# The recurrence of a time-mixing layer: four turned arrays and one product on ScalarE's banks, the product at another place

## The chip, the cores and the metric

One core of a Trainium2 chip. The metric is the device time of one execution in microseconds (us). Engines: TensorE (PE in the profile; PEld its weight loads), VectorE (DVE), ScalarE (ACT), GpSimd (POOL) and SyncE (SP), which issues DMAs.

## The reference, cut to what matters

The kernel computes one inference step of a two-layer hybrid decoder for 272 prompt tokens (16 of them learned) and 8 sample tokens. The change lies in the second layer, in the RWKV-7 recurrence over the prompt's 272 tokens, with 8 heads of 64:

```python
def wkv7(r, w, k, v, a, b, S0):
    def step(S, inp):
        r_t, w_t, k_t, v_t, a_t, b_t = inp
        sa = jnp.einsum('bhij,bhj->bhi', S, a_t)
        S = S * w_t[:, :, None, :] + sa[..., None] * b_t[:, :, None, :] + v_t[..., None] * k_t[:, :, None, :]
        return S, jnp.einsum('bhij,bhj->bhi', S, r_t)
```

The kernel does not step through tokens. It works by tiles of tokens: inside a tile the coupling of the tokens through `a` and `b` is a triangular system, whose inverse is built by doubling, and the state `S` goes forward by chunks of 32 tokens.

## The kernel before

Each engine has its own program; semaphores join them. All results of TensorE land in PSUM. Four banks (`VB`) are emptied by VectorE and four (`AB`) by ScalarE. Each set is a ring: TensorE's `claim()` takes the next bank and waits until it was freed four claims ago; `close(ring, ins, name)` tells the emptying engine that a bank is full and remembers under `name` the count at which it will be free again; `until(name)` waits for that. The emptying engine calls `take()` in the same order, so the order of an engine's emptying is that of TensorE's closing in its ring. On VectorE each step waits for its own end (`s.do`). `empty` (L1765 for VectorE, L2158 for ScalarE) copies one bank to scratch. In the profile, L1769 is VectorE's copy in `empty`, L1772 `mul`, L1775 `add`, L2160 ScalarE's copy.

The recurrence (TensorE from L543, VectorE from L937, ScalarE from L1150) runs over three tiles of 128, 128 and 16 tokens. Per tile:

- L546: four arrays (`ATF`, `BLF`, `KLF`, `XV`) are transposed to token rows, one bank each, and copied to `ATK`, `BLK`, `KLK`, `VTK` by VectorE. In tile 0 only, TensorE then transposes the shift rows (`sho`, L552, four banks of ScalarE), and VectorE waits for their copies before it writes `AKT`.
- L564: five pairs of products, a pair for even and odd heads, which VectorE masks into `NTM`, `TM_`, `AKT`, `RBT`, `RKT` (ten multiplications). Six more steps form the initial `TM_` and `TTM` (`t_init`), for which TensorE waits; GpSimd starts the sample rows' recurrence (L1238 on) from tile 0's.
- L567 to L588, four levels: for each parity a product `x` (L576) that VectorE masks into `XX`, then from it an update of `TM_` (L583, not in the last level) and one of `TTM` (L587, `t0` and `t1`), which VectorE adds.
- L590 to L593: `ak`, the strictly lower triangle `AKT` times the values `VTK`, 8 products in one bank that VectorE copies to `AK`.
- L594 to L601: after `until("t1")`, `ta` = `TTM` times `ATK`, and `tv` = `TTM` times `AK` (L600).
- L606: `re`. L620: per chunk of 32 tokens the products that become `GTM` and `CCM`; VectorE forms `GTM[:, c]` by a multiplication of a constant identity with a column of `PL`, then copies and adds from the bank.
- L629, L630, L638, L642: output and state, chunk by chunk; ScalarE copies the tile's output (`yw`, L1152). Then the next tile starts.

Behind the three tiles TensorE goes on with the attention of the same layer.

## Time and profile before

| | |
|---|---|
| median of 3 runs | 1148.06 us (1147.82, 1148.06, 1151.13) |
| profiled execution | 1146.33 us, span of its records 1144.6 us |
| PE busy | 988.4 us (86%) |
| DVE busy | 484.6 us (42%) |
| ACT busy | 216.3 us (19%) |
| POOL busy | 138.0 us (12%) |
| mean granted TensorE clock | 0.879 |
| the recurrence | 583.0 to about 737 us of the span |

Times in the trace are microseconds from the start of the span. Each row of a timeline merges equal instructions of one engine that follow one another: start, duration, engine, line, operation, tiles, shape, count, and in brackets how long the engine stood idle before it and what released it. Ends of matmuls are modelled, so that two rows of PE can overlap a little. PEclk is the granted TensorE clock: 1.00 is 2.4 GHz, 0.50 is 1.2 GHz.

### The profile page before, as it was taken

To read this page: it belongs to the slowest core of one execution; us is meant where nothing else is said; L and a number is where in the kernel's file an instruction comes from. 1 tells how busy PE (TensorE), PEld (TensorE's weight loads), DVE (VectorE), ACT (ScalarE), POOL (GpSimd) and SP (SyncE) were. 2 spreads that over 40 slices of the span, in tenths; PEclk is the share of its full clock that TensorE was granted. 3 is DMA by queue.
4 is the path that set the end of the run, shared out by engine and by line. 5 is a ranking of instruction groups with operands and counts; after the bars stand their busy time and mean duration, and the time that the engine had idled before them with its cause. 6 is when DMAs were issued, how large, how long until landed. Compare 5 with 4: busy or idle time off the path is not lost.

```text
span 1144.6 us, 17771 instructions
## 1 busy us (share of the span) xinstructions
PE 988.4 (86%) x7132; PEld 742.6 (65%) x7132; DVE 484.6 (42%) x1060; ACT 216.3 (19%) x462; POOL 138.0 (12%) x177
## 2 busy tenths in 40 slices
PE   6997478779799999899969778996888988999995
PEld 4775366557666666677759777754555767666674
DVE  1697723452431110214886675438663135111114
ACT  0112011201401101125520000031454032111103
POOL 0005001000040000000029600002720002200000
PEclk9998756779699999989989688596699987999998
DMA  9403101715169998032100100003722541999501
GB/s 310 168 24 37 34 1 42 265 42 198 60 254 385 394 400 242 1 120 89 53 14 1 40 1 2 7 1 113 204 64 74 184 184 51 376 389 398 220 1 38
DMA packets 77222, 156.88 MB, mean 137 GB/s; under 512 B 19605, under 2 KB 57549, under 8 KB 68215
## 3 DMA queue, kind: packets, MB, share of 16 engines
q1 hardware_dynamic: 67668, 148.28, 35.6%
q0 software_dynamic: 3760, 4.48, 1.8%
q10 hardware_dynamic: 5710, 2.96, 0.9%
q8 instruction: 58, 0.95, 0.3%
q14 instruction: 26, 0.21, 0.1%
HBM read 149.25 MB, written 5.27 MB: 135 GB/s over the span
## 4 chain that ended last, share of the span: by engine, by line
PE 70%; DVE 21%; DMA 3%; ACT 3%; issue 2%; SPq 0%; POOL 0%; DVEq 0%; ACTq 0%
PE bank L1686 10%; PE bank L1350 7%; DVE scratch L1772 7%; PE bank L1673 6%; PE bank L1746 5%; PE bank L1718 5%; PE bank L1603 5%; DVE scratch L1775 2%; PE bank L1464 2%; PE bank L576 2%; PE bank L1634 2%; PE bank L756 2%; DMA scratch<-u_tok_dram 1%; PE bank L1552 1%; PE bank L587 1%
## 5 line engine op out<-in xcount | busy, mean ns | idle before, releaser
L1350 PE MATMUL bank<-x_fm,weight_slots 128*128 128x280 f32 x576 | 143.0, 411 | 4.2 <-ACT x_fm L2228 2.8
L1350 PEld LDWEIGHTS bank<-x_fm,weight_slots 128*128 128x128 f32 x576 | 112.5, 196 | 32.9 <-issue 4.4
L2160 ACT ACTIVATE scratch<-bank 128x280 f32<-128x280 f32 (+5 forms) x118 | 52.9, 454 | 325.1 <-PE bank L1718 92.3
L1686 PE MATMUL bank<-weight_slots,scratch 128*64 128x256 f32 x672 | 92.5, 379 | 1.2 <-DVE scratch L1769 1.2
L1686 PEld LDWEIGHTS bank<-weight_slots,scratch 128*64 128x64 f32 x672 | 58.5, 137 | 27.8 <-issue 4.6
L1769 DVE COPY scratch<-bank 128x256 f32<-128x256 f32 (+5 forms) x108 | 55.9, 517 | 43.1 <-PE bank L1673 17.2
L1772 DVE TENSOR_TENSOR scratch<-scratch 128x64 f32<-128x64 f32 (+12 forms) x95 | 57.8, 626 | 33.9 <-ACT scratch L2160 31.4
L1673 PE MATMUL bank<-scratch 128*128 128x128 f32 x512 | 68.3, 289 | 0.0
L1772 DVE TENSOR_TENSOR scratch<-bank,scratch 128x256 f32<-128x256 f32 x16 | 6.8, 424 | 143.6 <-PE bank L1686 143.6
L1603 PE MATMUL bank<-scratch,weight_slots 128*128 128x280 f32 x256 | 63.5, 411 | 4.0 <-DVE scratch L1772 4.0
L1673 PEld LDWEIGHTS bank<-scratch 128*128 128x128 f32 x512 | 62.2, 199 | 4.1 <-issue 0.4
L1746 PE MATMUL bank<-scratch 128*128 128x280 f32 x256 | 60.9, 400 | 1.4 <-ACT scratch L2160 1.4
L1603 PEld LDWEIGHTS bank<-scratch,weight_slots 128*128 128x128 f32 x256 | 50.2, 197 | 17.0 <-DVE scratch L1772 4.4
L1746 PEld LDWEIGHTS bank<-scratch 128*128 128x128 f32 x256 | 48.5, 190 | 14.7 <-ACT scratch L2160 3.2
L1686 PE MATMUL bank<-scratch 128*64 128x256 f32 x352 | 56.9, 379 | 0.0
L1263 POOL DMA_DIRECT2D scratch<-in_cache_krope x64 | 34.4, 538 | 160.9 <-DVE residual L1017 143.6
L1686 PEld LDWEIGHTS bank<-scratch 128*64 128x64 f32 x352 | 35.7, 137 | 16.4 <-issue 3.4
L1207 POOL TENSOR_TENSOR scratch<-scratch 128x256 f32<-128x256 f32 x24 | 16.1, 704 | 241.3 <-DVE scratch L1772 241.3
L1464 PE MATMUL bank<-scratch 64*42 64x128 f32 x128 | 25.9, 418 | 22.1 <-DVE scratch L1775 22.1
L1718 PE MATMUL bank<-weight_slots,scratch 128*64 128x512 f32 x192 | 43.8, 598 | 0.3
L2221 ACT ACTIVATE scratch<-residual 128x280 f32<-128x280 f32 x32 | 11.7, 437 | 156.6 <-DVE residual L2018 156.6
L1772 DVE TENSOR_TENSOR scratch<-bank,consts 128x512 f32<-128x512 f32 (+5 forms) x69 | 33.7, 488 | 15.4 <-PE bank L576 11.7
(380 smaller groups left out, 1496.3 us busy)
## 6 DMA issues: line engine op xcount, KB each, us to landing
weight_slots<-in_moe_w_down SPq DMA_DIRECT2D x24, 1024.0 KB, 9.5
weight_slots<-in_moe_w_up SPq DMA_DIRECT2D x22, 1024.0 KB, 7.9
weight_slots<-in_moe_w_gate SPq DMA_DIRECT2D x20, 1024.0 KB, 7.2
scratch<-in_moe_w_gate SPq DMA_DIRECT2D x12, 1024.0 KB, 8.2
scratch<-in_moe_w_up SPq DMA_DIRECT2D x10, 1024.0 KB, 8.8
weight_slots<-in_od_w_in SPq DMA_DIRECT2D x9, 1024.0 KB, 5.8
weight_slots<-in_ev_w_in SPq DMA_DIRECT2D x8, 1024.0 KB, 11.9
scratch<-in_moe_w_down SPq DMA_DIRECT2D x8, 1024.0 KB, 10.0
```

Of the source, the lines that this page charges most:

```text
L576: ins = pe.matmul(heads(b, r)[:r, hp, :], NTM[:r, par, hp, 0:r], TM_[:r, par, hp, 0:r], start=True, stop=True)
L1263: pool.dma_start(CK[:, sm, pg, 256:288], a["cache_krope"][bass.ds(page[i], 1), 0].rearrange("o p c -> p (o c)")).then_inc(ev(f"cache_krope ...
L1350: ins = pe.matmul(b[:, 0:NT], w[:, k, P * m2:P * m2 + P], src[:, k, :], start=(k == 0), stop=(k == kt - 1))
L1464: ins = pe.matmul(b[0:HCOL, P * i:P * i + P], HS[lo:lo + SP_N, j, g // 2, :], CP[lo:lo + SP_N, j, g // 2, 1:CL + 1, :].rearrange("p l c -> ...
L1603: ins = pe.matmul(b[:, 0:NT], w[:, k0 + k, P * m2:P * m2 + P], src[:, k, :], start=(which == 0 and k == 0), stop=(which == 1 and k == 3))
L1673: ins = pe.matmul(b[:, f], XTM[:, t, 4 * half + c, :], slots(t, slice(0, P)), start=False, stop=(t == 1))
L1686: ins = pe.matmul(b[CAP * j:CAP * j + CAP, 0:DE], XG[:, q % 2, k, CAP * j:CAP * j + CAP], w[j][:, k, :], start=(k == 0), stop=(k == KD - 1))
L1718: ins = pe.matmul(b[CAP * j:CAP * j + CAP, :], HT[:, q % 2, f, CAP * j:CAP * j + CAP], w[j][:, f, 512 * h:512 * h + 512], start=(f == 0), ...
L1746: ins = pe.matmul(b[:, 0:NT], YG[:, q, P * m:P * m + P], DSPT[:, q, :], start=(q == 0), stop=(q == NQ - 1))
L1769: s.do(dve.tensor_copy(dst, src if len(dst.shape) == 2 else src.rearrange("p (a b) -> p a b", a=dst.shape[1])), v_free)
L1772: return dve.tensor_tensor(o, x, y, ALU.mult)
L2160: return act.activation(dst, b[:rows, 0:width], f, **kw).then_inc(ring.free, 1)
```

## The change

The four transposed arrays of each tile go to ScalarE's ring: TensorE claims from `A`, and ScalarE empties them, in tile 0 between its copies of the sample rows and those of the shift rows. `ak` goes to ScalarE's ring too, and TensorE computes it in level 0 of each tile, behind the two `x` products and ahead of what uses them, after a new wait for the copies of the turned arrays (`until("wkv_tok")`). VectorE's five copies per tile fall away. The number of instructions stays the same otherwise.

```diff
--- before.py
+++ after.py
@@ -541,10 +541,10 @@
             n_st = 0
             for tt, (c0, r) in enumerate(PT):
                 for src in (ATF, BLF, KLF, XV):
-                    b = V.claim()
+                    b = A.claim()
                     for m in range(4):
                         ins = pe.transpose(b[:r, P * m:P * m + P], src[:, m, c0:c0 + r], ident)
-                    close(V, ins, "wkv_tok")
+                    close(A, ins, "wkv_tok")
                 if tt == 0:
                     for q in range(0, RT_N, 4):
                         b = A.claim()
@@ -575,6 +575,12 @@
                         for hp in range(4):
                             ins = pe.matmul(heads(b, r)[:r, hp, :], NTM[:r, par, hp, 0:r], TM_[:r, par, hp, 0:r], start=True, stop=True)
                         close(V, ins, f"x{par}")
+                    if lev == 0:
+                        until("wkv_tok")
+                        b = A.claim()
+                        for h in range(WH):
+                            ins = pe.matmul(b[:r, WD * h:WD * h + WD], AKT[:r, h % 2, h // 2, 0:r], VTK[:r, WD * h:WD * h + WD], start=True, stop=True)
+                        close(A, ins, "ak")
                     for par in range(2):
                         until(f"x{par}")
                         if lev < 3:
@@ -587,10 +593,6 @@
                             ins = pe.matmul(heads(b, r)[:r, hp, :], XX[:r, par, hp, 0:r], TTM[:r, par, hp, 0:r], start=True, stop=True)
                         close(V, ins, f"t{par}")
 
-                b = V.claim()
-                for h in range(WH):
-                    ins = pe.matmul(b[:r, WD * h:WD * h + WD], AKT[:r, h % 2, h // 2, 0:r], VTK[:r, WD * h:WD * h + WD], start=True, stop=True)
-                close(V, ins, "ak")
                 until("t1")
                 for src, name in ((ATK, "ta"), (AK, "tv")):
                     if name == "tv":
@@ -935,9 +937,6 @@
                 s.do(mul(BON[:, m, :], b[:, 0:NT], XV[:, m, :]), v_free)
             n_st = 0
             for tt, (c0, r) in enumerate(PT):
-                for dst in (ATK, BLK, KLK, VTK):
-                    empty(dst[:r, :], 512, r)
-
                 def heads(b, n):
                     return b[:n, 0:4 * n].rearrange("p (h x) -> p h x", h=4)
 
@@ -965,7 +964,6 @@
                             s.do(add(TM_[:r, par, :, 0:r], TM_[:r, par, :, 0:r], heads(b, r)), v_free)
                         b = V.take()
                         s.do(add(TTM[:r, par, :, 0:r], TTM[:r, par, :, 0:r], heads(b, r)), v_free)
-                empty(AK[:r, :], 512, r)
                 empty(TA[:r, :], 512, r)
                 empty(TV[:r, :], 512, r)
                 b = V.take()
@@ -1144,10 +1142,14 @@
 
             for q in range(6):
                 empty(SROW2[0:NB, 512 * q:512 * q + 512], 512, rows=NB)
-            for q in range(0, RT_N, 4):
-                n = P * min(4, RT_N - q)
-                empty((SHO1 if q < 8 else SHO2)[0:NB + 1, P * (q % 8):P * (q % 8) + n], n, rows=NB + 1)
             for tt, (c0, r) in enumerate(PT):
+                for dst in (ATK, BLK, KLK, VTK):
+                    empty(dst[:r, :], 512, rows=r)
+                if tt == 0:
+                    for q in range(0, RT_N, 4):
+                        n = P * min(4, RT_N - q)
+                        empty((SHO1 if q < 8 else SHO2)[0:NB + 1, P * (q % 8):P * (q % 8) + n], n, rows=NB + 1)
+                empty(AK[:r, :], 512, rows=r)
                 b = A.take()
                 act.activation(YW[:, :, c0:c0 + r], b[:, 0:4 * r].rearrange("p (h x) -> p h x", h=4), ACT.Copy).then_inc(a_free, 1)
             for h in range(MH):
```

## Rows read from the trace of the kernel before

**Rows 1.** The page's chain of work that ended last, shares of the span by engine.

```profile
PE 70%; DVE 21%; DMA 3%; ACT 3%; issue 2%; SPq 0%; POOL 0%; DVEq 0%; ACTq 0%
```

**Rows 2.** Timeline, TensorE: start us, us, engine, line, operation, count, [idle before, releaser].

```profile
583.03 1.91 PE L546 MATMUL bank<-consts,scratch 128*128 128x128 f32 x16
...
586.39 2.06 PE L564 MATMUL bank<-scratch 64*128 64x128 f32 x32
...
648.54 3.67 PE L546 MATMUL bank<-consts,scratch 128*128 128x128 f32 x16
...
712.32 0.37 PE L564 MATMUL bank<-scratch 64*16 64x16 f32 x16
...
713.75 0.86 PE L564 MATMUL bank<-scratch 64*16 64x16 f32 x32 [1.06 <-DVE scratch L1769]
```

**Rows 3.** Timeline, VectorE, the heads of the three tiles.

```profile
587.66 7.22 DVE L1772 TENSOR_TENSOR scratch<-bank,consts 128x512 f32<-128x512 f32 x10 [1.06 <-PE bank L564]
...
653.84 1.42 DVE L1772 TENSOR_TENSOR scratch<-bank,consts 128x512 f32<-128x512 f32 x2 [0.82 <-PE bank L564]
...
710.78 2.82 DVE L1769 COPY scratch<-bank 16x512 f32<-16x512 f32 x4 [1.31 <-PE bank L546]
...
713.63 2.58 DVE L1772 TENSOR_TENSOR scratch<-bank,consts 16x64 f32<-16x64 f32 x10
```

**Rows 4.** Timeline, ScalarE, ahead of tile 0.

```profile
581.04 2.98 ACT L2160 ACTIVATE weight_slots<-bank 8x512 f32<-8x512 f32 x6 [3.59 <-PE bank L537]
```

**Rows 5.** Timeline, TensorE, level 0 of tile 0 and of tile 2.

```profile
599.33 3.75 PE L576 MATMUL bank<-scratch 128*128 128x128 f32 x16 [6.05 <-DVE scratch L1775]
...
602.87 1.91 PE L583 MATMUL bank<-scratch 128*128 128x128 f32 x8
...
718.54 0.39 PE L583 MATMUL bank<-scratch 16*16 16x16 f32 x8 [0.16 <-DVE scratch L1772]
```

**Rows 6.** Timeline, TensorE, behind the last level of tiles 0 and 2.

```profile
622.79 1.90 PE L592 MATMUL bank<-scratch 128*128 128x64 f32 x16
...
624.52 3.74 PE L600 MATMUL bank<-scratch 128*128 128x64 f32 x32
...
724.57 1.86 PE L592 MATMUL bank<-scratch 16*16 16x64 f32 x16
...
726.23 3.62 PE L600 MATMUL bank<-scratch 16*16 16x64 f32 x32
```

**Rows 7.** Timeline, VectorE, last addition to TTM in tiles 0 and 2.

```profile
623.06 0.69 DVE L1775 TENSOR_TENSOR scratch<-scratch,bank 128x512 f32<-128x512 f32 x1 [0.43 <-PE bank L587]
...
724.84 0.21 DVE L1775 TENSOR_TENSOR scratch<-scratch,bank 16x64 f32<-16x64 f32 x1 [0.28 <-PE bank L587]
```

**Rows 8.** Timeline, VectorE: forming GTM in tile 0, and once in tile 1.

```profile
635.50 0.56 DVE L1772 TENSOR_TENSOR scratch<-consts,scratch 128x256 f32<-128x256 f32 x1
...
637.01 1.09 DVE L1772 TENSOR_TENSOR scratch<-consts,scratch 128x256 f32<-128x256 f32 x1
...
639.05 1.53 DVE L1772 TENSOR_TENSOR scratch<-consts,scratch 128x256 f32<-128x256 f32 x1
...
698.97 0.42 DVE L1772 TENSOR_TENSOR scratch<-consts,scratch 128x256 f32<-128x256 f32 x1
```

**Rows 9.** Timeline, GpSimd, the sample rows' recurrence beside tile 0.

```profile
635.86 1.96 POOL L1247 TENSOR_TENSOR scratch<-scratch 128x1024 f32<-128x1024 f32 x1
...
637.90 2.40 POOL L1248 TENSOR_TENSOR residual<-residual,scratch 128x1024 f32<-128x1024 f32 x1
...
640.38 2.41 POOL L1249 TENSOR_TENSOR scratch<-residual,scratch 128x1024 f32<-128x1024 f32 x1
```

**Rows 10.** Timeline, TensorE, chunk products and first state step of tile 0.

```profile
633.71 1.01 PE L620 MATMUL bank<-scratch 32*64 32x64 f32 x41 [1.63 <-issue]
...
641.55 1.12 PE L638 MATMUL bank<-scratch 64*64 64x64 f32 x16 [3.17 <-DVE scratch L1775]
```

**Rows 11.** Windows: us, then PE, PEld, DVE, ACT, POOL busy, PEclk, DMA, GB/s.

```profile
632.00:634.00 2.00, 0.37 (x27) 0.29 (x28) 0.00 (x0) 0.00 (x0) 1.92 (x2) 0.65 0.00 0
```

## The prediction

> **What bounds the kernel now.** I read the page's chain first: TensorE holds 70% of it and VectorE 21% [rows 1]. Then the timeline of each engine over the recurrence, 583 to 741 us of the profile, in which three tiles (128, 128 and 16 tokens) run one after another. Three things are to be seen there.
>
> At the head of a tile, TensorE transposes (L546), then makes the products (L564), and VectorE empties the transposes and masks the products. VectorE was idle 1.06 us before the masks of tile 0 and 0.82 us before those of tile 1, and what it waited for was L564 [rows 3]. So the four copies of the turned arrays are over by then, and VectorE waits for TensorE. Only in tile 2 is it the reverse: copies from 710.78 to 713.60, masks at 713.63 with no idle [rows 3], and TensorE's L564 stood 1.06 us for a bank that a copy held [rows 2].
>
> In the levels TensorE works without a break. In tile 0 L583 starts (602.87) while the modelled end of L576 is at 603.08, with no idle shown [rows 5]; tile 1 repeats this. Before level 0, however, it stands 6.05 us for VectorE's masks and initial arrays [rows 5], and no part of the change shortens these.
>
> Behind the levels, `ak` (L592) starts as soon as the last L587 has been issued, and `ta` (L600) follows it [rows 6], while VectorE makes the last addition to TTM, on which `ta` depends, beside `ak` [rows 7]. So `ak` is now the cover of a latency.
>
> **The change part by part.** The profiled execution took 1146.33 us (span 1144.6, 1.7 us around it), the median of the three runs is 1148.06. I add the difference found in the trace to the median.
>
> (a) *Turned arrays to ScalarE.* VectorE loses four copies a tile. In tiles 0 and 1 this is worth 0: TensorE's start of L564 isn't held by them (no idle on its rows at 586.39 [rows 2]), and the masks follow L564. What covers them is TensorE's own work between the first transpose and the first product; without that cover the four would cost 2.82 us [rows 3]. In tile 2 the first mask could start where L564's first pair ends, 712.69 [rows 2], plus about 0.24 us (the distance from one engine's end to the other's start at the head of tile 0: its first 16 of 32 rows, half of 2.06 us, end at 587.42, mask at 587.66 [rows 2, 3]): 712.93 instead of 713.63, 0.70 us. But then the products come just in time. Four VectorE banks hold two pairs; the third pair waits for two masks of 0.258 us [rows 3] and needs 0.43 us itself (0.86 for two [rows 2]), so that masks 5 and 9 each come some 0.24 us late. I take a gain of 0.22, with 0 and 0.70 as bounds.
>
> On ScalarE's side, tile 0: its six copies of the sample rows run from 581.04 to 584.02, 0.50 us each [rows 4]; the four new ones end near 586.1, and only then is a bank free for the last of the `sho` transposes, which TensorE is ready to start at about 586.2. The products come behind it in program order. I take 0.1 us, bounds 0 and 0.3. The `sho` copies end near 588.2, while VectorE asks for them only at its fifth mask, 590.5 (587.66 plus four of 0.72 [rows 3]): no cost. In tiles 1 and 2 ScalarE has nothing else; its bank of `yw` is free before the fourth transpose claims it. The SP stores behind `sho` move 1 us later and nobody waits for them. The added wait for `wkv_tok` stands long after these copies: no cost.
>
> (b) *`ak` behind x0 and x1 of level 0.* There TensorE has no gap, so all of it is inserted: 1.73 us in tile 0 (622.79 to 624.52 [rows 6]), the same in tile 1. Both level 0s start at half clock, since 16 of L576 take 3.75 us and then speed up; I take the point where the clock rises as fixed in time, so that some of `ak` runs slow, and as much of L583 and L587 runs fast in its stead. In tile 2, 1.66 us (724.57 to 726.23 [rows 6]) less the idle of 0.16 and the pipelining there: about +1.42.
>
> (c) *`ak` gone from behind the levels.* The sum would be zero if the cover weren't lost. The last addition ends at 623.75 (623.06 + 0.69 [rows 7]), and TensorE can be at `ta` 0.10 us later, 623.85. Before, TensorE was free at 622.79 [rows 6]. So 1.06 us of the 1.73 come back as a stall: tile 0 +1.06, tile 1 +1.06. Tile 2: addition ends 725.05, `ta` at 725.15 instead of 726.23, -1.08, with (b) +0.34. VectorE's copy of `ak` vanishes between two waits for TensorE: 0. What is late next is `ta`, `tv`, `re` and the chunk products, all 1.06 us later.
>
> (d) *A step in tile 0 that turns 1.06 into 2.5.* After the products of the chunks VectorE forms GTM four times by a multiplication whose two inputs both lie in scratch and constants. In tile 1 one takes 0.42 us; in tile 0, beside GpSimd, 0.56, 1.09 and 1.53 [rows 8]. Against GpSimd's rows the rule is exact: the one begun at 637.01 ends at 638.10, 0.28 us after GpSimd's end at 637.82; the one begun at 639.05 ends at 640.58, 0.28 after 640.30 [rows 8, 9]. The one at 635.50 ends at 636.06, just as GpSimd's next begins at 635.86. So each waits for the GpSimd instruction that is under way. The next multiplication begins 0.95 us after the end of one, and TensorE's state step 0.97 us after the last (640.58 to 641.55 [rows 8, 10]). Now everything 1.06 later, GpSimd where it is (it started from tile 0's initial arrays, which don't move against it): the second begins at 636.56 and ends at 638.10, the third 639.05 to 640.58, the fourth begins at 641.53 and waits for GpSimd's end at 642.79 (640.38 + 2.41 [rows 9]), ends at 643.07, state step at 644.04. That is +2.49 in place of +1.06. It holds for any shift between 0.28 and 2.3 us.
>
> The Trainium skill ("SBUF — State Buffer", section "SBUF: two separate sides") says that VectorE and GpSimd share a port pair held for a whole instruction, that a VectorE operation with two SBUF inputs takes part in it, and that the loser fully blocks. The trace agrees, with the 0.28 us above each time; a notion of shared bandwidth would stretch the multiplications by a ratio and leave tile 0 at +1.06.
>
> Sum: 0.1 + 2.49 (tile 0), 1.06 (tile 1), 0.34 - 0.22 (tile 2) = +3.8 us, so 1148.06 + 3.8 = 1151.8. With the bounds of (a) it is +3.3 to +4.1; TensorE's clock adds more than that, since its full level comes and goes in this region. It fell inside the window 632 to 634 us (mean 0.65 [rows 11]) and tile 1's transposes ran at half level (3.67 us against 1.91 [rows 2]). A rise or fall one us earlier or later costs or gives half a us, and there are some five in the region: I allow 1.2 us to either side, 1150.6 to 1153.0. By the Trainium skill ("TensorE: Matmul & The Clock Gate", "What's actually happening") the monitor runs free and does not restart with the kernel, so the same code may get its clock at another point; no run shown here tells that.
>
> **The rivals.**
>
> 1. *Tile 0's step (d) doesn't come.* TensorE stands 1.63 us with no releaser in the middle of L620 [rows 10]. If that gap shrinks by over 0.8 us, the second multiplication begins early enough to end at 636.06 as before and tile 0 costs 0.1: +1.3, 1149.4. If the multiplications don't queue as I read them, tile 0 costs 1.16: +2.3, 1150.4. For: the gap has no cause in the profile. Against: nothing ahead of it changes in number, and the multiplications' ends fit three times.
> 2. *The half clock lasts longer.* A TensorE idle of 1.06 us behind the levels and a longer one before the state steps could keep the clock low further into tile 1's levels. A full-clock level lasts 5.6 us (L576 of level 0 alone took 3.75 at the half clock), so one more us to a whole level at half speed costs 1 to 2.8 more: 1152.8 to 1154.6. Against: before L576 TensorE stands 6.05 us anyway.
> 3. *The other side, by the clock.* If the gap in L620 vanishes, TensorE may stay busy enough to keep full clock past 632. Then tile 1's transposes take 1.91 in place of 3.67 (-1.8), four state steps (L638 took 1.12 us in the first [rows 10]) perhaps 0.4 less each, the first products 0.4 less: -3.8 together. With tile 0 at +0.1 and tiles 1 and 2 at +1.2 that is -2.5: 1145.6. [...] Little speaks for it.
> 4. *The relief reaches the path.* If VectorE's copies were what holds the tiles, -2.8 three times and -0.7 for each of two `ak` copies, against what (b) and (c) show: up to -9.8, 1138.3. The idle of 1.06 and 0.82 us before the masks [rows 3] speaks against it.
>
> **How the numbers follow.** Forecast 0.50; rival 1 0.24; rival 2 0.17; rival 3 0.05; rival 4 0.04. A measurement here tells 0.3% from no change, 3.4 us: the limit 1151.5 lies inside the forecast's own range, and I put 0.19 of its 0.50 below it. Faster: rival 4 and a part of 3, 0.05. Same: 0.19 + 0.24 + 0.04 = 0.47. Slower: 0.31 + 0.17 = 0.48. The range 1148.6 to 1154.6 takes in the forecast and rivals 1 and 2, and leaves out 3 and 4.
>
> **What would show it.** Masks start as late after L564 as before in tiles 0 and 1, and VectorE's idle before them grows by the copies. L583 of level 0 starts 1.7 us later after L576. Between the last L587 and `ta` TensorE idles about 1.0 us for VectorE. GTM's last multiplication of tile 0 ends 0.28 us behind a GpSimd end, and the state step starts about 2.5 us later than before. Wrong would be: masks that start earlier, `ak` that finds a gap, or a clock that falls elsewhere.

## The result, and the profile after

The changed kernel takes 1158.16 us in the median of 13 runs, against 1148.67 us for the kernel before in 13 runs beside them. The two medians lie 9.5 us apart; the ratio estimated from all these runs is 1.0068 [1.0049, 1.0087], which is 7.8 us (5.6 to 10.0), and by it I go. I had forecast 1151.8 us, 3.7 us more than the median then known. The sign was right, the size (+3.8 us) was half of what came, and the time lies above the range.

Two things make the profiles hard to read here. Executions of the kernel before spread from 1141.51 to 1154.04 us. And its code ahead of the recurrence, which the change doesn't touch, took 583.03 us in the profile before and 586.49 us after. So I compare stretches, not absolute times, and below I use four profiles of each kind where one could mislead.

The page of the changed kernel: busy time of the engines, and the shares of the chain of work that ended last (before: [rows 1]).

```profile
PE 996.2 (87%) x7132; PEld 748.8 (65%) x7132; DVE 474.9 (41%) x1045; ACT 224.1 (19%) x477; POOL 138.1 (12%) x177
PE 71%; DVE 22%; ACT 3%; issue 2%; DMA 2%; SPq 0%; DVEq 0%
```

VectorE has lost 9.7 us of work and ScalarE has 7.8 us more, as the change says. The chain still runs through TensorE. TensorE itself is 7.8 us longer busy with the same number of matmuls, and that is already the hint: the same matmuls take longer where the granted clock is lower.

TensorE's timeline in tile 0 of the changed kernel (start us, us, line, shapes, count, idle before with its releaser):

```profile
586.49 1.91 PE L546 MATMUL bank<-consts,scratch 128*128 128x128 f32 x16
...
589.86 2.06 PE L564 MATMUL bank<-scratch 64*128 64x128 f32 x32
...
602.80 3.75 PE L576 MATMUL bank<-scratch 128*128 128x128 f32 x16 [6.05 <-DVE scratch L1777]
606.35 3.51 PE L582 MATMUL bank<-scratch 128*128 128x64 f32 x16
609.65 2.02 PE L589 MATMUL bank<-scratch 128*128 128x128 f32 x8
...
630.70 3.79 PE L602 MATMUL bank<-scratch 128*128 128x64 f32 x32 [0.85 <-DVE scratch L1777]
...
648.80 1.12 PE L640 MATMUL bank<-scratch 64*64 64x64 f32 x16 [4.95 <-DVE scratch L1777]
```

The products (L564) start 3.37 us after the transposes, before 3.36 [rows 2]. `ak` (L582) now stands in level 0, whole, and for 3.51 us: the clock is at its half level there. Then `ta` (L602) has the stall that was expected, 0.85 us. From `ta` to the first state step it is 18.10 us, before 17.03 (624.52 to 641.55 [rows 6, 10]). From the first `x` to `ta` it is 27.90 us, before 25.19 [rows 5, 6].

VectorE's masks at the heads of the three tiles, changed kernel:

```profile
591.12 7.22 DVE L1774 TENSOR_TENSOR scratch<-bank,consts 128x512 f32<-128x512 f32 x10 [4.98 <-PE bank L564]
...
660.93 7.22 DVE L1774 TENSOR_TENSOR scratch<-bank,consts 128x512 f32<-128x512 f32 x10 [5.32 <-PE bank L564]
...
720.48 2.58 DVE L1774 TENSOR_TENSOR scratch<-bank,consts 16x64 f32<-16x64 f32 x10 [2.43 <-PE bank L564]
```

The idle before the masks was 1.06 and 0.82 us [rows 3] and is 4.98 and 5.32 now: what the copies and the waits between them took has become idle time of VectorE. In tiles 0 and 1 they had not been on the path.

### The profile page after: what moved, and what is told of

It is laid out like the page before. It is cut to its first block, busy times and chain, and to the rows that moved or that the text cites. A ratio compares the mean times of both kernels' runs of the same rounds, so it can differ in the third digit from the quotient of the medians.

```text
span 1151.6 us, 17759 instructions
## 1 busy us (share of the span) xinstructions
PE 996.2 (87%) x7132; PEld 748.8 (65%) x7132; DVE 474.9 (41%) x1045; ACT 224.1 (19%) x477; POOL 138.1 (12%) x177
## 4 chain that ended last, share of the span: by engine, by line
PE 71%; DVE 22%; ACT 3%; issue 2%; DMA 2%; SPq 0%; DVEq 0%
PE bank L1688 10%; DVE scratch L1774 7%; PE bank L1352 7%; PE bank L1675 6%; PE bank L1748 5%; PE bank L1720 5%; PE bank L1605 5%; DVE scratch L1777 3%; PE bank L1466 2%; PE bank L576 2%; PE bank L1413 2%; PE bank L1636 2%; PE bank L758 2%; PE bank L1554 1%; PE bank L593 1%
## 5 line engine op out<-in xcount | busy, mean ns | idle before, releaser
L2162 ACT ACTIVATE scratch<-bank 128x280 f32<-128x280 f32 (+5 forms) x133 | 61.1, 468 | 369.8 <-PE bank L1720 92.3
L1771 DVE COPY scratch<-bank 128x256 f32<-128x256 f32 (+6 forms) x93 | 45.6, 490 | 37.8 <-PE bank L1675 16.9
```

Source lines behind the costliest of these rows:

```text
L1771: s.do(dve.tensor_copy(dst, src if len(dst.shape) == 2 else src.rearrange("p (a b) -> p a b", a=dst.shape[1])), v_free)
L2162: return act.activation(dst, b[:rows, 0:width], f, **kw).then_inc(ring.free, 1)
```

## The experiments

Columns of the table: the ratio to the kernel before with its 95% interval; the stretch of the recurrence in the profiled execution, from the first transpose (L546) to the first matmul of the next stage (`pe.matmul` on `uk`, L662 before and L664 after); and the stretch from there to the end of the span.

| kernel | edit | ratio | recurrence, us | behind it, us |
|---|---|---|---|---|
| before | | 1 | 154.8 | 406.8 |
| after | | 1.0068 [1.0049, 1.0087] | 158.7 | 406.4 |
| e1 | before again | 1.0005 [0.9982, 1.0027] | 153.3 | 406.9 |
| e2 | after again | 1.0072 [1.0046, 1.0098] | 155.9 | 410.4 |
| e3 | turned arrays alone | 0.9993 [0.9965, 1.0021] | 152.9 | 407.3 |
| e4 | `ak` alone | 1.0083 [1.0054, 1.0113] | 161.5 | 410.8 |
| e5 | after, `ak` in level 1 | 1.0054 [1.0031, 1.0078] | 160.7 | 410.5 |
| e6 | after, `ak` ahead of level 0 | 0.9960 [0.9938, 0.9982] | 149.3 | 409.0 |
| e7 | e6, `ta` even heads first | 0.9954 [0.9929, 0.9978] | 151.9 | 406.3 |
| e8 | after, `ta` even heads first | 1.0011 [0.9986, 1.0037] | 156.0 | 409.1 |
| e9 | before, no GpSimd recurrence | 0.9978 [0.9954, 1.0001] | 150.9 | 409.3 |
| e10 | after, no GpSimd recurrence | 1.0016 [0.9992, 1.0039] | 157.0 | 410.7 |
| e11 | before, +1.7 us in tile 2 | 0.9998 [0.9980, 1.0016] | 155.0 | 405.3 |
| e12 | before, +2.9 us in tile 2 | 1.0000 [0.9977, 1.0024] | 155.7 | 406.3 |
| e13 | before, +1 us behind it | 1.0029 [1.0005, 1.0053] | 153.8 | 412.5 |
| e14 | before, +2.5 us behind it | 1.0007 [0.9986, 1.0029] | 153.0 | 408.8 |
| e15 | after again | 1.0052 [1.0026, 1.0078] | 158.9 | 410.9 |
| e16 | after again | 1.0077 [1.0052, 1.0102] | 159.5 | 410.3 |

**Both kernels once more (e1, e2).**

> The kernel before, unchanged, timed against itself. All theories: ratio 1.000 within 0.2%. The stretch from the first L546 of tile 0 to the first L662 (recurrence) was 154.8 us in the profile of before; I expect 154 to 157. In the profiles compared so far 3.3 us of 7.0 arose at L1411 of the first layer, where TensorE's clock rose at 103.5 us in one and at 113.8 us in the other: if that is chance of the execution (theory A), this profile may show either; if it comes from the changed program (theory B), it shows the early rise again.

> The changed kernel again. Theory A (recurrence costs about 4 us, the rest chance of the clock): ratio 1.0035 to 1.007, recurrence 158 to 161 us. Theory B (the changed program costs 3 us more in the first layer): ratio near 1.007 with the late rise at L1413 again and the recurrence at 158.7 us. Theory C (product ak, at half the clock, holds off the clock's rise in level 0): the rise in tiles 0 or 1 comes later after the start of level 0 than the 6.0 and 4.6 us of before; one such delay costs some 1.7 us.

The loss stands on other executions too: 1.0072, and 1.0005 for the control. But the second profile of after has 25.61 us from the first `x` to `ta` of tile 0, not 27.90, and 410.4 us behind the recurrence, not 406.4. So one profile alone would have told a wrong story of where the time goes.

**The two halves (e3, e4).** In e3 the turned arrays go to ScalarE and `ak` stays where it was:

```diff
                 for src in (ATF, BLF, KLF, XV):
-                    b = V.claim()
+                    b = A.claim()
...
-                    close(V, ins, "wkv_tok")
+                    close(A, ins, "wkv_tok")
...
+                until("wkv_tok")
                 b = V.claim()
                 for h in range(WH):
                     ins = pe.matmul(b[:r, WD * h:WD * h + WD], AKT[:r, h % 2, h // 2, 0:r], VTK[:r, WD * h:WD * h + WD], start=True, stop=True)
```

In e4 (the same lines of the changed kernel turned back to `V`) the turned arrays stay on VectorE, and `ak` is in level 0 on ScalarE's bank.

> Only the four turned arrays go to ScalarE's banks; ak stays on VectorE's bank behind the levels. My sum: tile 0 +0.1, tile 1 0, tile 2 -0.2 to -0.7: -0.1 to -0.6 us, ratio 0.999 to 1.000. Rival (the copies on VectorE held the tiles): -3 to -8 us. Rival (ScalarE's queue delays the products): +1 to +3 us.

> Only ak goes to level 0 and to ScalarE's bank; the turned arrays stay with VectorE. My sum: tile 0 +2.5 (1.06 lost cover, then the wait for GpSimd), tile 1 +1.06, tile 2 +0.34: +3.9 us, ratio 1.0034. Theory C adds 1.7 to 3.4 us for a late clock: ratio up to 1.006. Rival (the turned arrays on ScalarE are what costs): ratio 1.000 to 1.001.

The turned arrays alone change nothing that can be measured (0.9993), and `ak` alone costs as much as the whole change (1.0083). e3 also shows tile 2. Its VectorE and TensorE timelines at the head of tile 2:

```profile
714.05 2.58 DVE L1773 TENSOR_TENSOR scratch<-bank,consts 16x64 f32<-16x64 f32 x10 [2.99 <-PE bank L564]
```

```profile
713.58 0.57 PE L564 MATMUL bank<-scratch 64*16 64x16 f32 x32
...
714.65 0.86 PE L564 MATMUL bank<-scratch 64*16 64x16 f32 x32 [0.50 <-DVE scratch L1773]
```

TensorE does wait 0.50 us with its third pair of products, and still VectorE's ten masks run 2.58 us on end, no longer than before [rows 3]. The wait is covered. The masks begin 0.47 us after the first product here, and 1.31 us after it in the kernel before (712.32 to 713.63 [rows 2, 3]).

**Where `ak` stands, and the stall behind the levels (e5 to e8).**

e5 moves `ak` one level on:

```diff
-                    if lev == 0:
+                    if lev == 1:
```

e6 takes it out of the level and puts it ahead of the waits for the initial arrays, behind a wait for the products that it reads:

```diff
+                    if lt is KTF and rt is ATF:
+                        mark["akt"] = mark["prod1"]
 
+                until("akt")
+                until("wkv_tok")
+                b = A.claim()
+                for h in range(WH):
+                    ins = pe.matmul(b[:r, WD * h:WD * h + WD], AKT[:r, h % 2, h // 2, 0:r], VTK[:r, WD * h:WD * h + WD], start=True, stop=True)
+                close(A, ins, "ak")
                 for par in range(2):
                     pe.wait_ge(ev("t_init"), 2 * tt + par + 1)
...
-                    if lev == 0:
...
```

e7 (on e6) and e8 (on after) start `ta` with the heads whose TTM is ready earlier:

```diff
-                until("t1")
+                until("t0")
...
-                    for h in range(WH):
+                    for h in ((0, 2, 4, 6, 1, 3, 5, 7) if name == "ta" else range(WH)):
+                        if name == "ta" and h == 1:
+                            until("t1")
```

> The changed kernel with ak in level 1 instead of level 0, so that it no longer runs while TensorE's clock is at its lower level after the 6 us idle. The stretch from the first L546 to L662 was 154.8 and 153.3 us in two profiles of before, 158.7, 155.9 and (ak alone moved) 161.5 us with ak in level 0. Theory R (ak in the slow phase holds off the clock's rise): as the changed kernel less 1.7 to 3.4 us, ratio to before 1.003 to 1.006. Theory E (the loss lies behind the levels: the lost cover, the wait for GpSimd, an earlier fall of the clock there): as the changed kernel, ratio 1.006 to 1.008, stretch 156 to 161 us.

> The changed kernel with ak ahead of level 0, behind the products, where TensorE stands 6 us for VectorE. ak costs nothing there, but the cover behind the levels stays lost. Sum against before: tile 0 and tile 1 -0.67 each (-1.73 of ak, +1.06 of stall), tile 2 -1.1 and -0.9 from the turned arrays: -3 us, stretch about 151.5, ratio 0.997. Theory E with a large loss behind the levels (earlier fall of the clock): ratio 0.999 to 1.004. Theory R: the clock in level 0 rises as in before, ratio below 1.

> As the run before, and ta computes its four even heads first, which need only the even half of TTM, so that they cover the last addition to the odd half. Sum against before: -1.6 in tiles 0 and 1, -1.5 in tile 2, -0.9 from the turned arrays: -5 us, ratio 0.9955, TensorE idle ahead of ta's odd heads below 0.3 us. Theory E (a fall of the clock behind the levels, because nothing dense stands there): 1 to 3 us less gain, ratio 0.997 to 0.999.

> The changed kernel with the even heads of ta first: only the stall behind the levels is mended. My sum: +0.2 in tiles 0 and 1 and no wait for GpSimd beyond that of before, tile 2 -1.1: ratio 0.999 to 1.001, stretch 154. Theory R (loss in level 0's slow phase): still +2 to +5 us, ratio 1.002 to 1.005. If the whole loss stays (1.007), neither the stall nor the wait for GpSimd is what costs.

Level 1 is no better a place than level 0 (1.0054 with an interval that overlaps that of after). The gap ahead of level 0 is: e6 is faster than the kernel before, 0.9960. TensorE in e6, tile 0:

```profile
594.88 2.00 PE L574 MATMUL bank<-scratch 128*128 128x64 f32 x16
...
601.00 1.41 PE L584 MATMUL bank<-scratch 128*128 128x128 f32 x5 [4.12 <-DVE scratch L1779]
```

`ak` takes 2.00 us out of the idle time, and 4.12 us of it are left before the first `x`.

e7 adds the other order of the heads to e6; 0.9954 and 0.9960 can't be told apart.

Taking away the stall of 0.85 us alone, with `ak` still inside level 0 (e8), brings the ratio from 1.0072 to 1.0011, which is some 7 us. In the same place:

```profile
604.72 3.51 PE L582 MATMUL bank<-scratch 128*128 128x64 f32 x16
...
628.07 3.90 PE L604 MATMUL bank<-scratch 128*128 128x64 f32 x32
```

`ta` (L604) has no idle before it any more. But the three stalls are only 0.85, 0.85 and 0.37 us long, 2.1 us in all (the changed kernel's waits, columns: waiting line and what it waits for, total us, count, longest). So the stalls cost more than their length, some three times it. What the rest is made of stands below, as far as the traces show it.

```profile
PE bank L640 <- DVE scratch L1777: 7.4, 2, 5.0
PE bank L602 <- DVE scratch L1777: 2.1, 3, 0.8
```

**The step beside GpSimd (e9, e10).** Both leave out the recurrence of the sample rows on GpSimd, so the outputs that come from it aren't computed; the kernels' other work is the same.

```diff
-                s.do(tt(TS, st, q_[0], ALU.mult))
...
-                row_sums(SYS[:, hs], ev("sys_ready"))
+                s.do(tt(SAS[:, hs], SVV[:, hs], SVV[:, hs], ALU.mult), ev("wks_ready"))
+                s.do(tt(SYS[:, hs], SVV[:, hs], SVV[:, hs], ALU.mult), ev("sys_ready"))
```

> The kernel before with the sample rows' recurrence on GpSimd left out (its outputs for the samples' state and values are not computed). It serves as the base for the next run. If VectorE's GTM multiplications of tile 0 wait for GpSimd's instructions, all four take 0.42 us here, and from the start of ta to the first state step tile 0 takes about 13.0 us as tile 1 does, plus the unexplained idle in L620 of about 1.6 us where it appears (before: 17.0 and 17.7): 13 to 15. Rival (the multiplications are slow for another reason): 0.5 to 1.5 us each as before.

> The changed kernel with the same part left out. Against the run before, tile 0 is longer by 1.06 us for the stall, plus 1.7 where the clock rises a step later in level 0, and by nothing for GpSimd: ta to first state step equal in both within 0.2 us. Ratio of this to the base without GpSimd 1.004 to 1.007; if GpSimd's part were large, it would be below 1.003.

Without GpSimd each multiplication of tile 0 takes what it takes in tile 1 (0.42 us [rows 8]). VectorE in e9, then in e10, one of the four that form GTM:

```profile
634.67 0.43 DVE L1765 TENSOR_TENSOR scratch<-consts,scratch 128x256 f32<-128x256 f32 x1
```

```profile
643.45 0.42 DVE L1767 TENSOR_TENSOR scratch<-consts,scratch 128x256 f32<-128x256 f32 x1
```

So GpSimd is what lengthens them. The distance between the two kernels is then 0.0038 instead of 0.0068 or 0.0072. The difference of these differences is about 3 to 4 us, but each ratio is uncertain by 2.2 to 3 us, so it doesn't measure step (d) by itself; the rows do, below. The forecast of e10 for this stretch missed: from `ta` to the state step of tile 0 it is 15.51 us against 14.78 in e9, and not the same within 0.2. The clock fell 8.8 us after `ta` in e10 and 14.2 us after it in e9, so that more of this stretch ran at the half level; that this is the reason is argued and not tested.

**More work, no change of the recurrence (e11 to e14).** e11 and e12 compute the last state product of tile 2 three and five times, e13 and e14 add two and five matmuls of 0.49 us in the next stage. The edits of e11 and of e13 (e12 and e14 have a 5 in place of the 3 and the 2):

```diff
-                    for h in range(WH):
+                    for h in list(range(WH)) * (3 if tt == 2 else 1):
...
+                for k in range(2 if h == 6 else 0):
+                    pe.matmul(b[0:64, 0:NT], w[:, 0, 96 * (h % 4):96 * (h % 4) + 64], QAN[:, 0, :], start=True, stop=True)
```

> The kernel before with the last state product of tile 2 computed three times instead of once: about 1.8 us more work at one place behind the recurrence, nothing else. In ten profiles the stretch behind the recurrence (first L662 to the end) took 406.3 to 407.3 us where TensorE's clock rose 3.5 to 4.1 or 1.1 us after it began, and 409.0 to 410.8 where it rose 1.5 to 2.8 us after. Theory L (a shift of the work against the clock's own grid costs time far downstream): this kernel rises 2.2 us after, the stretch takes 409 to 411, ratio 1.003 to 1.005. Rival (the downstream difference is chance of the execution): +1.8 us, ratio 1.0016.

> As the run before with five computations, 3.6 us more work. Theory L: the shift has gone once round, the rise comes near 3.8 us after the stretch begins, which takes 406 to 407: ratio 1.003, no more than with the delay of 1.8 us. Rival (chance): +3.6 us, ratio 1.0032, twice that of the run before. The two theories differ in the run before, and in the order of the two.

> The kernel before with two matmuls of 0.49 us each repeated in the attention's projections behind the recurrence, at TensorE's full clock. Fourteen profiles can be sorted by where the stretch behind the recurrence lies against the steps of the clock: start of L662 less half of the slow time that follows it, counted from a step. From 2.85 by way of 0 to 1.77 us the stretch took 405.3 to 407.3 us, from 1.89 to 2.66 it took 409.0 to 410.8. The kernel before stood at 1.40 and 1.37 in two profiles; 0.98 us more puts it at 2.4. Theory L (the place against the clock's steps decides): stretch 410 to 412, ratio 1.003 to 1.005. Rival (executions fall anywhere, the place is not set by the kernel): +1.0 us, ratio 1.001.

> The same with five repeats, 2.45 us of work. Theory L: from 1.4 to 3.85, once round to 0.44: only the work itself, stretch 409.3, ratio 1.002, less than the run before. Rival: ratio 1.002, more than the run before's 1.001.

I wanted to know whether the loss behind the recurrence comes from the mere delay, by where the work then meets the steps of TensorE's clock. In the form that I had given it, this theory failed in e11 and e12: the added work cost nothing that can be measured (0.9998 and 1.0000). The last state product in e11 and in e12, where 1.12 us stood before (735.13 in the profile of before):

```profile
736.74 2.83 PE L638 MATMUL bank<-scratch 64*64 64x64 f32 x48
```

```profile
737.54 4.05 PE L638 MATMUL bank<-scratch 64*64 64x64 f32 x80
```

That is 1.7 and 2.9 us more. The reason why it is not seen is in the matmuls behind it. TensorE in e11, then in e13, which has the recurrence of before:

```profile
740.63 1.91 PE L662 MATMUL bank<-consts,weight_slots 128*64 128x128 f32 x16
```

```profile
739.69 3.62 PE L662 MATMUL bank<-consts,weight_slots 128*64 128x128 f32 x16
```

With the extra products in front, the first matmuls behind the recurrence run at the full clock, 1.91 us in place of 3.62 (in e12 too), and that alone gives back 1.7 us. Over all timed runs e11 and e12 spend 286 and 284 us at half clock, the kernel before beside them 290 (how this is worked out stands below). From the start of that state product to the first matmul on L670 it is 6.22 us in before, 5.73 in e11 and 6.95 in e12. So the added work costs -0.5 and +0.7 us there, and neither can be seen in a ratio that is uncertain by 2 us or more.

e13 and e14 delay the rest without that. The forecasts, on record before they ran, were a stretch of 410 to 412 us in e13 and 409.3 in e14, though e14 adds more; measured were 412.5 and 408.8. Windows of e13, then of e14 (us, then busy time of PE, PEld, DVE, ACT, POOL, the granted clock, DMA share, GB/s):

```profile
880.00:900.00 20.00, 16.76 (x220) 9.71 (x213) 6.27 (x14) 2.04 (x6) 0.00 (x0) 0.92 0.65 221
900.00:920.00 20.00, 20.00 (x79) 15.80 (x78) 1.82 (x5) 0.00 (x0) 0.00 (x0) 0.91 0.40 144
```

```profile
880.00:900.00 20.00, 16.77 (x233) 9.38 (x232) 6.14 (x14) 4.10 (x10) 0.00 (x0) 1.00 0.61 211
900.00:920.00 20.00, 20.00 (x87) 16.11 (x85) 2.36 (x6) 0.00 (x0) 0.00 (x0) 1.00 0.44 158
```

In e13 the clock falls to its half level on both sides of 900 us; in e14 it doesn't. Less the work that was added (0.98 and 2.45 us) the stretches are 411.5 and 406.4. This supports the theory in its second form. The ratios stand in the order forecast, 1.0029 and 1.0007, but their intervals overlap, so they don't settle it.

The sorting that the forecast of e13 speaks of holds in all eighteen profiles. Take the start of L662, add half of the half-level time right behind it (the figures of that forecast come out with this half added; it says "less") and the added work of e13 and e14, and count from the clock's steps in the same trace. The seven profiles at 1.0 to 1.8 us have no extra spell at the half level (before, after, e1, e7, e11, e12, e14), the ten at 1.9 to 2.8 us have it (e2, e4, e5, e6, e8, e9, e10, e13, e15, e16), and e3 at 2.85 us has none there and a shorter one at 835 to 839 us. Four of them, e13 to e16, ran after the rule was on record.

**The changed kernel twice more (e15, e16).**

> The changed kernel again, for another profile. Theory F (with the stall behind the levels the clock falls early in some executions): in tile 1 from ta to the first state step either 13.1 us (no fall) or 15.8 to 16.2 us (the clock falls within 3 us of ta's start), as in one and three of the profiles with ak inside a level. From the first x product to ta in tile 0 either 25.6 or 27.9 us, by the clock's step in level 0. Rival: a value between.

> The same once more. If both copies show 13.1 us in tile 1, the early fall belongs to rarer executions and does not carry the median.

In tile 1 it is 13.08 us from `ta` to the first state step in e15 (no fall of the clock) and 15.65 in e16 (a fall), and in tile 0 25.6 us from the first `x` to `ta` in both, close to the two-valued forecasts.

With them I have four profiles of the changed recurrence (after, e2, e15, e16) and four with the old one (before, e1, e13, e14). Means of the parts:

| part, us | old | changed | difference |
|---|---|---|---|
| tile 0, first `x` to `ta` | 24.87 | 26.18 | +1.31 |
| tile 0, `ta` to state step | 17.38 | 18.24 | +0.86 |
| tile 1, head | 16.10 | 16.66 | +0.56 |
| tile 1, first `x` to `ta` | 24.66 | 25.46 | +0.80 |
| tile 1, `ta` to state step | 13.03 | 14.44 | +1.41 |
| tile 1, state steps | 6.35 | 6.56 | +0.21 |
| tile 2, head | 8.06 | 6.99 | -1.07 |
| tile 2, first `x` to `ta` | 8.44 | 8.91 | +0.47 |
| the whole recurrence | 153.71 | 158.26 | +4.5 |

Behind the recurrence the changed kernel needs 409.5 us on average (406.4, 410.4, 410.9, 410.3), the kernel before 406.8 and 406.9, which is +2.65. Together that is +7.2 us, and the timed runs say +7.8.

## Why the prediction was too low

**(a) Turned arrays: right in tiles 0 and 1, mis-sized in tile 2.** e3 shows it alone, and the idle of 4.98 and 5.32 us before the masks shows why nothing comes of it. ScalarE's late bank cost nothing in tile 0 (3.37 against 3.36 us to the products), where I had put 0.1. In tile 2 I took -0.22 with -0.70 as the bound, because I had VectorE waiting at its masks 5 and 9. It does not (2.58 us on end in after and in e3), and the head of tile 2 became 1.07 us shorter. That is past the bound too: the first product itself had stood behind a copy, and the masks follow it after 0.47 us and not after 0.61. e3 and e11 go through tile 2's head at the same clock, and there it is 6.96 against 8.14 us. The term was mis-sized by 0.85 us, and not to the side of the miss: with its true size the forecast would have been lower still. (The bounds that the sum names, +3.3 to +4.1, are +3.2 to +4.2 when they are added up.)

**(b) `ak` inside level 0: right in kind.** I forecast +1.73 in tile 0 and tile 1, less the 1.73 us that had stood behind the levels, plus the stall of 1.06. That is +1.06 from the first `x` to `ta`. The means are +1.31 and +0.80; that their mean is 1.06 is partly luck, since the clock stands in both. Profiles whose clock steps alike give it cleanly: 25.62, 25.62 and 25.59 us in tile 0 of e2, e15 and e16 against 24.50 and 24.54 in e1 and e13, which is +1.09. In tile 2 it was +0.47 for a forecast of +0.34.

**(c) The stall: right.** It came as 0.85 us of idle in front of `ta` in tiles 0 and 1 and 0.37 in tile 2.

**(d) GpSimd: the rule right, and the landing a matter of tenths of a us.** VectorE's multiplications in tile 0 of the changed kernel, then GpSimd's rows beside them:

```profile
641.68 2.27 DVE L1774 TENSOR_TENSOR scratch<-consts,scratch 128x256 f32<-128x256 f32 x1
...
644.90 1.53 DVE L1774 TENSOR_TENSOR scratch<-consts,scratch 128x256 f32<-128x256 f32 x1
...
647.38 0.45 DVE L1774 TENSOR_TENSOR scratch<-consts,scratch 128x256 f32<-128x256 f32 x1
```

```profile
641.31 2.36 POOL L1250 TENSOR_TENSOR residual<-residual,scratch 128x1024 f32<-128x1024 f32 x1
643.75 2.40 POOL L1251 TENSOR_TENSOR scratch<-residual,scratch 128x1024 f32<-128x1024 f32 x1
```

The first ends at 643.95, 0.28 us after GpSimd's 643.67; the second at 646.43, 0.28 after 646.15; the third finds no long GpSimd instruction and takes 0.45. So the multiplications do queue as I had read them, and e9 and e10 show that GpSimd is the cause. (One reading was off: the multiplication at 635.50 [rows 8] ends 0.28 us behind a GpSimd instruction too, the one before the rows shown.)

Read from the first `x` of tile 0, the queue sets the time of the state step: 42.2 to 42.3 us in all seven profiles that have the old recurrence and GpSimd's, though `ta` starts anywhere from 24.5 to 25.2 us. I had forecast 2.49 us more. e15 and e16 have 44.6 (+2.4), and so have e4, e5 and e8 (44.7); after, with its late clock, has 46.0, and e2 has 42.4. e2 and e15 start `ta` at the same 25.62 us and part at the second multiplication. VectorE and GpSimd in e2, then in e15:

```profile
638.73 0.42 DVE L1774 TENSOR_TENSOR scratch<-consts,scratch 128x256 f32<-128x256 f32 x1
638.78 2.14 POOL L1249 TENSOR_TENSOR scratch<-scratch 128x1024 f32<-128x1024 f32 x1
```

```profile
639.53 1.90 POOL L1249 TENSOR_TENSOR scratch<-scratch 128x1024 f32<-128x1024 f32 x1
639.67 2.04 DVE L1774 TENSOR_TENSOR scratch<-consts,scratch 128x256 f32<-128x256 f32 x1
```

In e2 VectorE begins 0.05 us before GpSimd and takes 0.42 us; in e15 it begins 0.14 us behind it and takes 2.04. The difference comes from the idle inside L622 that no releaser explains, 1.70 us in e2 and 1.84 in e15. So "it holds for any shift between 0.28 and 2.3 us" was wrong, and rival 1, which let that gap decide, came true in one profile of four (+0.2 us in tile 0, where it had put 0.1). The mean over the four is +2.2 us from `x` to the state step, for a forecast of +2.49: +1.31 up to `ta` and +0.86 behind it, which are not independent of each other.

**The step that failed is the clock's allowance, "I allow 1.2 us to either side".** It treated the clock as noise around the sum, from "some five" steps of half a us; the trace of before has nine steps between 583 and 738 us. And it gave the 407 us behind the recurrence nothing. Inside the recurrence the means say +4.5 us for the +3.8 of the sum, so that there the allowance held, in part because the gain in tile 2 and the landing in e2 stand against the clock's losses. With +2.65 us behind the recurrence it did not. The clock went one way in three places, and the third lies outside the region that I looked at.

First, *the late rise in level 0*. Two windows of after, the first with the clock still at half level, the second behind its rise, and below them one of before that ends its level 0 at the full clock:

```profile
608.00:610.00 2.00, 2.00 (x11) 2.00 (x11) 0.00 (x0) 0.10 (x1) 1.76 (x4) 0.50 0.00 0
...
612.00:614.00 2.00, 2.00 (x19) 2.00 (x19) 1.28 (x3) 0.00 (x0) 1.92 (x2) 0.95 0.00 0
```

```profile
605.00:607.00 2.00, 2.00 (x19) 2.00 (x18) 1.29 (x3) 0.00 (x0) 1.84 (x3) 0.93 0.00 0
```

The rise comes 9.4 us after the first `x` in after, and 4.5 to 6.1 us after it in before and every profile with the old recurrence. I had written "I take the point where the clock rises as fixed in time"; with `ak` in the level it comes late in 3 of 7 profiles (after, e8, e10) and costs 1.65 us then up to `ta` (27.90 against 25.19 + 1.06). These three had seen the clock fall 4.3 us ahead of the first `x`. Three without `ak` in level 0 had too (before, e14, e5, 4.2 to 4.3 us), and theirs rose 6.0 to 6.1 us after it. Where it had fallen 2.2 to 2.4 us ahead, it rose after 4.5 to 4.7 us, with `ak` (e2, e4, e15, e16) or without. So `ak` delays the rise, and does it only when the clock fell early.

Second, *the early fall in tile 1*. TensorE in e16, then in e1, behind the levels of tile 1:

```profile
693.65 4.58 PE L602 MATMUL bank<-scratch 128*128 128x64 f32 x32 [0.85 <-DVE scratch L1777]
698.16 1.98 PE L608 MATMUL bank<-scratch 128*64 128x128 f32 x16
701.09 3.24 PE L622 MATMUL bank<-scratch 32*64 32x64 f32 x192 [0.95 <-DVE scratch L1777]
```

```profile
688.49 3.74 PE L600 MATMUL bank<-scratch 128*128 128x64 f32 x32
692.16 1.09 PE L606 MATMUL bank<-scratch 128*64 128x128 f32 x16
694.20 2.27 PE L620 MATMUL bank<-scratch 32*64 32x64 f32 x192 [0.95 <-DVE scratch L1775]
```

The same instructions, 4.58, 1.98 and 3.24 us in place of 3.74, 1.09 and 2.27. The clock falls 2.2 to 2.8 us after `ta` starts; the window in e16 shows it on the way:

```profile
696.00:698.00 2.00, 2.00 (x13) 2.00 (x12) 0.45 (x1) 0.00 (x0) 0.00 (x0) 0.61 0.00 0
```

It happens in 5 of 7 profiles that have both the stall and `ak` in a level (e2, e16, e4, e5, e10), each time for 2.6 to 3.1 us, and in none of ten without the stall. That the stall does it is likely and not shown, since the ten differ in more than the stall: by the clock's steps, nine of them start tile 1's `ta` at another place than the five do. Only e7 stands where e5 and e10 stand, to 0.05 us, and it has no fall; so one profile speaks for the stall against the mere place. And the place matters: e16 has the fall, e15, the same kernel 0.02 us away, has not. e6 has the stall but `ak` in the gap, and one profile of it without the fall; whether the fall needs both is open.

This accounts for a part of what e8 gives back, not for all of it. The stalls are 2.1 us and five falls in seven profiles some 2 us on average, of 7. The rest isn't traced to a place; but e8's timed runs spend 291 us at the half clock, as the kernel before beside them does (290), and those of the changed kernel 295 to 301, so that it too is with the clock. Rival 2 had named this mechanism ("a TensorE idle of 1.06 us behind the levels ... could keep the clock low") and put it in tile 1's levels at 1 to 2.8 us. It lies behind them, and it came in half of the four profiles of the changed kernel, for the 0.17 that I gave it.

Third, *behind the recurrence*, where no instruction has changed, +2.65 us. The stretch is 409 to 412.5 us where the clock has an extra spell at its half level between 883 and 910 us (e2, e4, e5, e6, e8, e9, e10, e13, e15, e16), and 405 to 407.3 where it has none (before, after, e1, e3, e7, e11, e12, and e14 less what it adds). e16, then e1:

```profile
900.00:920.00 20.00, 20.00 (x76) 15.73 (x76) 1.78 (x4) 0.00 (x0) 0.00 (x0) 0.88 0.38 132
```

```profile
900.00:920.00 20.00, 20.00 (x86) 16.10 (x86) 3.12 (x7) 0.00 (x0) 0.00 (x0) 1.00 0.46 158
```

Three of the four profiles of after have it, and neither of the two of before. That the place of the work against the clock's steps decides it is well supported, by e13 and e14 and by the sorting of all eighteen profiles; by e11 and e12 it isn't the delay as such. Why three in four of the changed kernel's executions land badly is open. And the size, +2.65, rests on two profiles of before that are on the light side: they spend 277 and 279 us at the half clock, and the kernel's timed runs 288 on average (worked out next). So some of its timed runs probably have the spell too, and 2.65 is more likely too large than too small.

All this shows in the timed executions too. Twice (1 - mean granted clock) times the span is the time at half clock. It averages 288 us over the 34 timed runs of the kernel before beside e2, and 301, 296, 295 and 300 us in after, e2, e15 and e16; in e6 it is 280. The 7 to 13 us more are matmuls at half speed, beside which other work also stands, so that not all of it lengthens the span. As an estimate from the means above, 2 to 3 of the 7.2 us are the four terms at the size that they had, and 4 to 5 us stand where the sum had no term.

The Trainium skill ("TensorE: Matmul & The Clock Gate", "What's actually happening") says that the monitor runs free of the kernel's start. The traces agree as far as they go: code ahead of the change, the same in all these kernels, ended anywhere between 579.8 and 588.6 us. What I should have drawn from it is that a sum from one profile holds one case of several in each of its clock-bound parts.

## What to carry to other kernels

Work that covers a latency is not free to move: behind it comes a stall, and stalls of 0.85 us in front of narrow matmuls cost about three times their length here (e8), probably by way of TensorE's clock. Move it only into a real gap (e6 and e7: 0.9960 and 0.9954, against 1.0072), or close the stall in the same change by starting with the halves that are ready (e8: 1.0011). When you price a change near steps of the clock, ask of each new idle and each inserted instruction in the slow phase which way it can push a step, price that to one side, and compare several profiles, over the whole span and not the changed region alone.

## What the runs showed of the hardware that I had not expected

Added matmuls can be nearly free: 2.9 us of them at the end of tile 2 gave 1.0000 [0.9977, 1.0024], while the time at half clock fell from 290 to 284 us. A VectorE multiplication with two inputs in SBUF ended 0.27 to 0.30 us behind the GpSimd instruction that was under way wherever the two met in the profiles that I read, and stood for up to 2.27 us in place of 0.42; whether it began 0.05 us before GpSimd's or 0.14 us behind it made 0.42 or 2.04 us of it. The Trainium skill ("SBUF — State Buffer", "SBUF: two separate sides") calls this an exclusive lock, and the rows agree. And 2.5 us more work behind the recurrence made the rest of the kernel no slower than 1 us more did (1.0007 and 1.0029, intervals overlapping).
